# One tile of a depthwise convolution's 31 taps moved from VectorE to GpSimd

## The chip, the cores and the metric

The kernel runs on one core of one Trainium2 chip. The metric is the device time of one execution in microseconds; several executions are made and the median is quoted. The profiled execution is one more of them, with its own time. In the profile PE is TensorE, DVE is VectorE, ACT is ScalarE, POOL is GpSimd and SP is SyncE, whose queue issues the weight transfers.

## The reference, cut to what matters

The program computes two transformer-like blocks on 256 tokens of width 1024. The first block has two layers (DEPTH = 2), each a mixer and a feed-forward part. The mixer joins an mLSTM branch (four heads) with a convolution branch; the convolution branch is what the change touches:

```python
a = glu_a * jax.nn.sigmoid(glu_b)
a = causal_depthwise_conv(a, w_dw, b_dw)            # 31 taps, each channel by itself
a = jax.nn.silu(group_layer_norm(a, N_CONV_GROUPS, g_cn, b_cn))
return jnp.concatenate([h_m, a], axis=-1) @ w_out   # h_m: the mLSTM branch, gated
```

Output t of a channel is its bias plus the sum over back = 0..30 of weight(back) times input t - back. The second block (attention, a merge, and a retrieval of experts' rows by index) follows and is not touched but for the names of some semaphores.

## The kernel before, in words

Everything is float32. Activations are held with channels on the 128 partitions and the 256 tokens along a row, so 1024 channels are eight tiles of 128x256. Weights stream through a ring of four 1 MB buffers filled by the SP queue. Each engine runs a list of instructions written out by hand in the order of the source, and semaphores join them; nothing reorders them.

U is a buffer of 32 tiles. In a mixer, U[16..23] first hold glu_a and U[24..31] the sigmoid of glu_b. `long_conv(l, pair)` (line 1461) is VectorE's work on two tiles: one multiplication makes the gated input in U[24..] for both (line 1466), and then for each of the 31 taps `tap` (line 1446) issues one instruction per tile. Tap 0 is a TENSOR_SCALAR (line 1453), taps 1 to 30 are SCALAR_TENSOR_TENSOR (line 1456): shifted input times a per-channel weight plus the running sum, written back to U[16..]. Each tap waits for the tap before it on the same tile, so two tiles taken in turn keep the engine from standing still. VectorE's order in a layer is: pairs 0, 1, 2 of the long convolution, the short convolution of the mLSTM branch (4 taps, 8 tiles, `short_conv`), pair 3, the gate logarithms (lines 1532 to 1537), then for each of four heads the decay weights, the scores, and a quotient written to tmp[2h, 2h+1] (line 1556), and then the norms. tmp has eight tiles; early in the layer it holds the weights wvT that TensorE reads at line 573.

TensorE meanwhile does the input projection (lines 540 and 553), the value, query and key products (594, 584), the gates (610), more projection (540), the four heads (632 to 649), the mLSTM norm (659 to 668), the first half of the output projection (678), and only then waits for the convolution (`conv_ready`) and sums its tiles for the group norm (688). ScalarE moves results out of the accumulators (1051), applies silu to the short convolution (1096), and prepares the gates (1105 to 1116).

GpSimd issues DMAs. In the second layer its list reads: the load of mem_2; a wait for the last of the heads (`head_done`); two small loads; a wait for the mixer; wgn and wcmp; and so on.

Of the kernel before, what the change touches and what calls it, by code (L numbers as in the profile page):

```python
# [12 lines left out]
P = 128  # L13
# [160 lines left out]
def build_program(nc, a, out):  # L174
    ctx = ExitStack()
    with ctx:
# [220 lines left out]
        def _(pool):  # L397
# [36 lines left out]
            pool.wait_ge(sem("mod_kept"), 5)  # L434
            pool.dma_start(memtok, a["mem_2"][0].rearrange("(s p) d -> p s d", p=P)).then_inc(sem("mem_in"), 16)
            pool.wait_ge(sem("head_done"), H * DEPTH)
            pool.dma_start(onehot[0:N_BUCKETS, :], a["onehot"]).then_inc(sem("bias_in"), 16)
# [4 lines left out]

            pool.wait_ge(sem("bias_masked"), 1)
            pool.wait_ge(sem("bias_copied"), 1)
            pool.dma_start(bias_dram.rearrange("p h u -> h p u"), bias_w[0:NH, :].unsqueeze(1).broadcast_to([NH, P, 512])).then_inc(sem("bias_out"), 16)
# [6 lines left out]
            pool.wait_ge(sem("memT_ready"), 1)  # L452
            pool.dma_start(rc, a["rcount"].partition_broadcast(P)).then_inc(sem("rcount_in"), 16)
            pool.wait_ge(sem("x_ready"), 2 * DEPTH * CT)
            pool.dma_start(wcmp[1], a["wcmp"][1]).then_inc(sem("wcmp_in"), 16)
            pool.dma_start(wpg[:, :, :], a["wpg"]).then_inc(sem("wpg_in"), 16)
            pool.wait_ge(sem("pooled"), 1)
# [22 lines left out]
        def _(pe):  # L480
# [81 lines left out]
            for l in range(DEPTH):  # L562
# [122 lines left out]

                pe.wait_ge(sem("conv_ready"), 4 * (l + 1))
                for c in range(CT):
                    i = nc.tensor.matmul(st[:, c, :], ones[:, :], U[:, 16 + c, :], start=True, stop=True)
                    if c % 2:
                        i.then_inc(sem("gn_summed"), 1)  # L690
# [24 lines left out]
                for j in range(16):  # L715
                    w = ring_slot(("w_ff2", l, j)).rearrange("p (k n) -> p k n", n=P)
                    if l == DEPTH - 1 and j == 4:
                        pe.wait_ge(sem("mem_scaled"), 1)
                        for c in range(CT):
                            for s in range(2):  # L720
                                i = nc.tensor.transpose(st[:, c, P * s:P * s + P], memtok[:, s, P * c:P * c + P], ident[:, :])
                        i.then_inc(sem("mem_turned"), 1)
                        pe.wait_ge(sem("bias_in"), 32)
                        nc.tensor.matmul(ms[1][0:NH, :, :].rearrange("p a t -> p (a t)"), rel[0:N_BUCKETS, :], onehot[0:N_BUCKETS, :],
                                         start=True, stop=True).then_inc(sem("bias_made"), 1)
                    if j % 2 == 0:
                        b = take_bank()
                    for k in range(16):
                        kk = 16 * (j % 2) + k
                        i = nc.tensor.matmul(b[:, 0, :], w[:, k, :], U[:, kk, :], start=(kk == 0), stop=(kk == 31))  # L730
                    i.then_inc(sem("slot_used"), 1)
# [140 lines left out]
            for u in range(len(UNITS)):  # L872
                if u + 1 < len(UNITS):
                    scores(u + 1)
                for name in FILL[u]:
                    if name == "mix":
                        pe.wait_ge(sem("wpg_in"), 16)
# [124 lines left out]
        def _(act):  # L1002
# [81 lines left out]
            for l in range(DEPTH):  # L1084
# [83 lines left out]
                for c in range(CT):  # L1168
                    drain_y(l, 3, c, ("w_ff2", l, 2 * c + 1))
                    if l == DEPTH - 1 and c == 1:  # L1170
# [3 lines left out]
                        i.then_inc(sem("memT_ready"), 1)  # L1174
                        act.wait_ge(sem("bias_made"), 1)
                        nc.scalar.copy(bias_w[0:NH, 0:T], ms[1][0:NH, 0, :]).then_inc(sem("bias_copied"), 1)
                norm_pair(2 * l + 1)
# [128 lines left out]
            for s in range(2):  # L1306
                act.wait_ge(sem("acc_made"), s + 1)
                link(nc.scalar.activation(h_tok[:, s, :], acc[:, s, :], ACT.Square, accum_out=mstat[:, 0, s:s + 1]))
                nc.scalar.activation(mstat[:, 1, s:s + 1], mstat[:, 0, s:s + 1], ACT.Sqrt, bias=eps_col[:, 0:1], scale=1.0 / D).then_inc(sem("tok_std"), 1)
                for hf in range(2):  # L1310
# [36 lines left out]
            for s in range(2):  # L1347
                act.wait_ge(sem("v_used"), (2 * PH - 1 + s) * TOPK)
                link(nc.scalar.activation(h_tok[:, s, :], acc[:, s, :], ACT.Square, accum_out=mstat[:, 0, s:s + 1]))
                nc.scalar.activation(mstat[:, 1, s:s + 1], mstat[:, 0, s:s + 1], ACT.Sqrt, bias=eps_col[:, 0:1], scale=1.0 / D).then_inc(sem("last_std"), 1)  # L1350

        @block.vector
        def _(dve):
# [108 lines left out]
            def long_conv(l, pair):  # L1462

                a, b = U[:, 16 + 2 * pair:18 + 2 * pair, :], U[:, 24 + 2 * pair:26 + 2 * pair, :]
                dve.wait_ge(sem("proj_drained"), 60 * l + (2 * pair + 2 if pair < 3 else 16))
                link(nc.vector.tensor_tensor(b, a, b, ALU.mult))
                for back in range(KC):
                    tap(l, U[:, 16:24], U[:, 24:32], KC, W_DW, B_DW, back, (2 * pair, 2 * pair + 1), "conv_ready" if back == KC - 1 else None)

# [47 lines left out]
            for l in range(DEPTH):  # L1517
# [22 lines left out]
                for h in range(H):  # L1540
# [13 lines left out]
                    link(nc.vector.tensor_tensor(den[:, :], den[:, :], en_b[:, :], ALU.max))  # L1554
                    link(nc.vector.reciprocal(den[:, :], den[:, :]))
                    nc.vector.tensor_tensor(tmp[:, 2 * h:2 * h + 2, :], st[:, 6:8, :], den[:, :].unsqueeze(1).broadcast_to([P, 2, T]), ALU.mult).then_inc(sem("head_done"), 1)

# [43 lines left out]
                if l == DEPTH - 1:  # L1601
# [7 lines left out]

                    nc.vector.memset(bias_w[0:NH, T:512], NEG).then_inc(sem("bias_masked"), 1)  # L1610
                sum_pair(2 * l + 1)
# [29 lines left out]
            for u, (g, s) in enumerate(UNITS):  # L1641
# [24 lines left out]
                if u == 1:  # L1666

                    dve.wait_ge(sem("pool_kept"), 1)
                    dve.wait_ge(sem("cmp_made"), 1)
                    dve.wait_ge(sem("rcount_in"), 16)  # L1670
                    src = poolT
# [41 lines left out]
            def norm_tokens(s):  # L1713

                dve.wait_ge(sem("tok_std"), s + 1)
                link(nc.vector.reciprocal(mstat[:, 1, s:s + 1], mstat[:, 1, s:s + 1]))
# [72 lines left out]
            for s in range(2):  # L1789
                dve.wait_ge(sem("last_std"), s + 1)  # L1790
                link(nc.vector.reciprocal(mstat[:, 1, s:s + 1], mstat[:, 1, s:s + 1]))
# [27 lines left out]
```

## Time and profile before

| what | value |
|---|---|
| median of three runs | 2181.64 us (2178.7 to 4809.78) |
| profiled execution, its own time | 2180.84 us |
| its span, first to last instruction | 2179.1 us |
| PE busy | 1952.1 us (90% of the span) |
| DVE busy | 1050.0 us (48%) |
| ACT busy | 491.5 us (23%) |
| POOL busy | 314.1 us (14%) |
| mean granted TensorE clock | 0.966 of full speed |

Between the span and the execution's own time lie 1.7 us. A share of busy time is an average over very different stages: in the first half of the program TensorE works nearly without a gap, in the last third the row transfers of the retrieval set the pace. What an edit in one stage is worth is read from that stage.

### The profile page before, as it was taken

Reading aid. Unit: us, or ns where it says so; the run is one execution under the profiler, and the core shown is the slowest. Engines: PE = TensorE matmul, PEld = TensorE weight load, DVE = VectorE, ACT = ScalarE, POOL = GpSimd, SP = SyncE. Lnnn points to the kernel's source line nnn. Section 1 sums busy time; section 2 is a strip of 40 time slices with the busy share of each in tenths; the row PEclk is TensorE's granted clock in tenths of the full one; section 3 lists DMA queues with packets and bytes.
Section 4 is the critical chain, followed back from the end, with each engine's and each line's share of the span. In section 5 each row is a group of like instructions: output and inputs, shape, how many; then the busy total and the mean of one; then the engine's idle time right before and its main releaser. Section 6 shows DMA issues by size and latency. Waiting matters only on the chain.

```text
span 2179.1 us, 20885 instructions
## 1 busy us (share of the span) xinstructions
PE 1952.1 (90%) x7920; PEld 1433.0 (66%) x7920; DVE 1050.0 (48%) x2553; ACT 491.5 (23%) x1198; POOL 314.1 (14%) x328
## 2 busy tenths in 40 slices
PE   4998899999999899999999999998887888888776
PEld 4877688888786687888888777787443433433332
DVE  6993566500796422001200322223777767677754
ACT  2023221100113222120010344312213213222222
POOL 1000001000000000000000000001444344344441
PEclk9999899999999999999999999999999999999999
DMA  9712169944341143449542222245999999999996
GB/s 401 277 57 78 42 267 414 377 151 148 134 188 39 40 177 117 155 140 248 206 155 97 107 78 77 78 155 225 392 423 421 421 421 413 414 422 421 421 421 283
DMA packets 71715, 517.38 MB, mean 237 GB/s; under 512 B 8128, under 2 KB 8384, under 8 KB 11456
## 3 DMA queue, kind: packets, MB, share of 16 engines
q0 software_dynamic: 45808, 326.65, 37.6%
q1 hardware_dynamic: 25808, 189.40, 23.1%
q8 instruction: 63, 1.03, 0.2%
q14 instruction: 36, 0.29, 0.0%
HBM read 510.78 MB, written 5.24 MB: 237 GB/s over the span
## 4 chain that ended last, share of the span: by engine, by line
PE 71%; DMA 13%; DVE 10%; ACT 4%; issue 1%; SPq 0%; POOL 0%; DVEq 0%; ACTq 0%; POOLq 0%
PE pj L540 17%; DMA region<-in_peer_uv,small 10%; PE pj L730 9%; PE pj L745 9%; PE st L997 8%; PE pj L678 5%; DVE region L1778 3%; PE pj L553 3%; PE pj L965 2%; PE pj L584 1%; PE pj L757 1%; PE pj L774 1%; PE pj L864 1%; DMA pe_T<-in_pe_cols 1%; DMA ring<-in_ring_w 1%
## 5 line engine op out<-in xcount | busy, mean ns | idle before, releaser
L997 PE MATMUL st<-region 128*128 128x512 f32 x940 | 447.4, 625 | 118.3 <-ACT region L1340 118.2
L997 PEld LDWEIGHTS st<-region 128*128 128x128 f32 x940 | 179.9, 198 | 375.2 <-issue 196.2
L540 PE MATMUL pj<-hT,ring 128*128 128x256 f32 x1792 | 392.9, 381 | 1.0 <-ACT region L1159 1.0
L540 PEld LDWEIGHTS pj<-hT,ring 128*128 128x128 f32 x1792 | 340.9, 191 | 49.1 <-ACT region L1159 1.8
L1778 DVE CUSTOM_DVE_ANT_0 region<-region 128x1024 f32<-128x1024 f32 x235 | 285.6, 1224 | 107.1 <-DMA region<-in_peer_uv,small 104.0
L475 POOL DMA_INDIRECT region<-in_peer_uv,small x235 | 254.8, 1084 | 394.7 <-PE st L997 328.7
L730 PE MATMUL pj<-region,ring 128*128 128x256 f32 x1024 | 222.1, 379 | 3.6 <-ACT region L1159 2.7
L730 PEld LDWEIGHTS pj<-region,ring 128*128 128x128 f32 x1024 | 194.2, 190 | 31.9 <-ACT region L1159 3.5
L1456 DVE SCALAR_TENSOR_TENSOR region<-region,pc 128x255 f32<-128x255 f32 (+19 forms) x528 | 202.8, 473 | 0.0
L1340 ACT ACTIVATE region<-ident,small 128x128 f32<-128x128 f32 x256 | 88.8, 394 | 381.6 <-DVE small L1786 381.6
L1408 DVE TENSOR_TENSOR tmp<-xT,hT 128x256 f32<-128x256 f32 x32 | 13.6, 425 | 260.0 <-ACT hT L1072 260.0
L1482 DVE CUSTOM_DVE_ANT_0 region<-region 128x1024 f32<-128x1024 f32 x96 | 113.0, 1222 | 53.4 <-DMA region<-in_ada_rest 40.2
L745 PE MATMUL pj<-hT,ring 128*128 128x256 f32 x576 | 128.8, 384 | 0.6 <-ACT region L1249 0.6
L745 PEld LDWEIGHTS pj<-hT,ring 128*128 128x128 f32 x576 | 109.9, 192 | 16.3 <-issue 1.2
L678 PE MATMUL pj<-region,ring 128*128 128x256 f32 x448 | 106.5, 402 | 4.9 <-DVE region L1568 4.9
L678 PEld LDWEIGHTS pj<-region,ring 128*128 128x128 f32 x448 | 90.8, 204 | 21.1 <-issue 7.2
L1051 ACT ACTIVATE region<-pj 128x512 f32<-128x512 f32 x56 | 33.5, 597 | 225.1 <-PE pj L540 173.4
L553 PE MATMUL pj<-hT,ring 128*128 128x256 f32 x256 | 64.3, 418 | 18.2 <-ACT hT L1064 18.2
L432 POOL DMA_DIRECT2D region<-in_ada_rest x40 | 21.4, 535 | 384.2 <-DVE mod_sum L1482 362.2
L1072 ACT ACTIVATE hT<-pj,mod_scale 128x256 f32<-128x256 f32 x30 | 14.2, 474 | 275.1 <-PE pj L730 204.6
L553 PEld LDWEIGHTS pj<-hT,ring 128*128 128x128 f32 x256 | 54.1, 213 | 29.7 <-issue 21.0
L745 PE MATMUL pj<-region,ring 128*128 128x256 f32 x320 | 70.2, 380 | 2.6 <-DVE region L1636 1.9
(321 smaller groups left out, 1958.6 us busy)
## 6 DMA issues: line engine op xcount, KB each, us to landing
ring<-in_ring_w SPq DMA_DIRECT2D x161, 1024.0 KB, 4.8
region<-in_ada_rest POOLq DMA_DIRECT2D x40, 1024.0 KB, 12.3
region<-in_ada_first SPq DMA_DIRECT2D x4, 2048.0 KB, 17.6
region<-in_wqkv SPq DMA_DIRECT2D x2, 3072.0 KB, 12.2
region<-in_wcmp POOLq DMA_DIRECT2D x2, 2048.0 KB, 8.6
bias_dram<-region POOLq DMA_DIRECT2D x1, 4096.0 KB, 46.5
region<-in_peer_uv,small POOLq DMA_INDIRECT x235, 16.5
tmp<-in_wvT SPq DMA_DIRECT2D x2, 1024.0 KB
```

What stands on the lines that cost most here:

```text
L475: nc.gpsimd.indirect_dma_start(out=uv[n % NBUF], out_offset=None, in_=a["peer_uv"], in_offset=bass.IndirectOffsetOnAxis(ap=ids[:, n:n + 1] ...
L540: i = nc.tensor.matmul(b[:, m, :], w[:, k, P * m:P * m + P], hT[:, k, :], start=(k == 0), stop=(k == CT - 1))
L553: i = nc.tensor.matmul(b[:, m, :], w[:, k, P * m:P * m + P], hT[:, k, :], start=(k == 0 and m == 0), stop=(k == CT - 1 and m == 1))
L678: i = nc.tensor.matmul(b[:, 0, :], w[:, k, :], U[:, 8 + k, :], start=(k == 0), stop=(k == 15))
L730: i = nc.tensor.matmul(b[:, 0, :], w[:, k, :], U[:, kk, :], start=(kk == 0), stop=(kk == 31))
L745: i = nc.tensor.matmul(b[:, n, :], w[:, k, P * m:P * m + P], src[:, k, :], start=(k == 0), stop=(k == k_tiles - 1))
L965: i = nc.tensor.matmul(b[:, m, :], w[:, k, P * m:P * m + P], hT[:, k, :], start=(k == 0), stop=(k == CT - 1))
L997: i = nc.tensor.matmul(acc[:, u % 2, 512 * hf:512 * hf + 512], diag[:, m % NDIAG, :], uv[m % NBUF][:, D + 512 * hf:D + 512 * hf + 512], st ...
L1340: nc.scalar.activation(diag[:, m % NDIAG, :], ident[:, :], ACT.Copy, scale=wgt[:, u, k:k + 1]).then_inc(sem("diag_ready"), 1)
L1456: i = nc.vector.scalar_tensor_tensor(dst[:, c, back:T], src[:, c, 0:T - back], wc, dst[:, c, back:T], ALU.mult, ALU.add)
L1482: nc.vector.tensor_tensor_reduce(w, w, c_act, 1.0, 0.0, ALU.mult, ALU.add, mod_sum[:, ada_at:ada_at + 1]).then_inc(sem("ada_used"), 1)
L1778: nc.vector.tensor_tensor_reduce(row, row, h_tok[:, u % 2, :], 1.0, 0.0, ALU.mult, ALU.add, dots[:, u, k:k + 1]).then_inc(sem("u_used"), 1)
```

## The change: what it does

In the second layer (l = 1) the long convolution of tile 5 is taken out of VectorE's pair 2 and done on GpSimd. VectorE still multiplies the gated input for both tiles of the pair and then signals `glu_ready`; its taps of that pair are those of tile 4 alone. GpSimd has no fused form here: tap 0 is one TENSOR_SCALAR, and each of taps 1 to 30 is a product into tmp[7] (TENSOR_SCALAR) and an addition to U[21] (TENSOR_TENSOR), with a wait on GpSimd's own semaphore between each instruction and the next. GpSimd starts when `glu_ready` has come and TensorE has finished with wvT in tmp (`wvg_made`). Two waits on the end of this work are new: VectorE's last head quotient, which overwrites tmp[7], and TensorE's group sums. The other edits join pairs of semaphores into one; in one of them VectorE, in the second block, now waits for the load of wpg as well as for that of rcount (`pool_in` at 32).

```diff
@@ gpsimd, after the load of mem_2
+            pool.wait_ge(sem("glu_ready"), 1)
+            pool.wait_ge(sem("wvg_made"), DEPTH)
+            l, c = DEPTH - 1, 5
+            for back in range(KC):
+                wc = pc[:, l, W_DW + (KC - 1 - back) * CT + c:W_DW + (KC - 1 - back) * CT + c + 1]
+                if back == 0:
+                    nc.gpsimd.tensor_scalar(U[:, 16 + c, :], U[:, 24 + c, :], wc, pc[:, l, B_DW + c:B_DW + c + 1], ALU.mult, ALU.add).then_inc(sem("pool_tap"), 1)
+                    continue
+                pool.wait_ge(sem("pool_tap"), back)
+                nc.gpsimd.tensor_scalar(tmp[:, 7, back:T], U[:, 24 + c, 0:T - back], wc, None, ALU.mult).then_inc(sem("pool_product"), 1)
+                pool.wait_ge(sem("pool_product"), back)
+                nc.gpsimd.tensor_tensor(U[:, 16 + c, back:T], U[:, 16 + c, back:T], tmp[:, 7, back:T], ALU.add).then_inc(sem("pool_conv_ready" if back == KC - 1 else "pool_tap"), 1)
             pool.wait_ge(sem("head_done"), H * DEPTH)
@@ tensor, before the group sums
                 pe.wait_ge(sem("conv_ready"), 4 * (l + 1))
+                if l == DEPTH - 1:
+                    pe.wait_ge(sem("pool_conv_ready"), 1)
@@ vector, long_conv
-                link(nc.vector.tensor_tensor(b, a, b, ALU.mult))
+                i = nc.vector.tensor_tensor(b, a, b, ALU.mult)
+                tiles = (2 * pair, 2 * pair + 1)
+                if l == DEPTH - 1 and pair == 2:
+                    link_to(i, "glu_ready", 1)
+                    tiles = tiles[:1]
+                else:
+                    link(i)
                 for back in range(KC):
-                    tap(l, U[:, 16:24], U[:, 24:32], KC, W_DW, B_DW, back, (2 * pair, 2 * pair + 1), "conv_ready" if back == KC - 1 else None)
+                    tap(l, U[:, 16:24], U[:, 24:32], KC, W_DW, B_DW, back, tiles, "conv_ready" if back == KC - 1 else None)
@@ vector, the heads' quotient
+                    if l == DEPTH - 1 and h == H - 1:
+                        dve.wait_ge(sem("pool_conv_ready"), 1)
                     nc.vector.tensor_tensor(tmp[:, 2 * h:2 * h + 2, :], st[:, 6:8, :], den[:, :].unsqueeze(1).broadcast_to([P, 2, T]), ALU.mult).then_inc(sem("head_done"), 1)
@@ vector, the second block
-                    dve.wait_ge(sem("rcount_in"), 16)
+                    dve.wait_ge(sem("pool_in"), 32)
```

On GpSimd the work comes between the load of mem_2 and the load of onehot. In a row stand the line, the operation, what it writes and reads (tmp, and region, of which U is a part) and what it waits for. Before:

```order
24 L435 DMA region<-in_mem 128x2x1024 [waits mod_kept]
25 L437 DMA region<-in_onehot 32x512 [waits head_done]
26 L438 DMA region<-in_rel_bias 32x16
27 L440 DMA small<-in_wgn 128x384 [waits mix_ready]
28 L441 DMA region<-in_wcmp 128x4096
```

After, its beginning and its end (rows 30 to 82 repeat the pair of product and addition, one element shorter each time):

```order
24 L435 DMA region<-in_mem 128x2x1024 [waits mod_kept]
25 L442 TENSOR_SCALAR region<-region,pc 128x256 [waits wvg_made,glu_ready]
26 L445 TENSOR_SCALAR tmp<-region,pc 128x255 [waits pool_tap]
27 L447 TENSOR_TENSOR region<-region,tmp 128x255 [waits pool_product]
28 L445 TENSOR_SCALAR tmp<-region,pc 128x254 [waits pool_tap]
29 L447 TENSOR_TENSOR region<-region,tmp 128x254 [waits pool_product]
...
84 L445 TENSOR_SCALAR tmp<-region,pc 128x226 [waits pool_tap]
85 L447 TENSOR_TENSOR region<-region,tmp 128x226 [waits pool_product]
86 L449 DMA region<-in_onehot 32x512 [waits head_done]
87 L450 DMA region<-in_rel_bias 32x16
88 L452 DMA small<-in_wgn 128x384 [waits mix_ready]
```

So 61 instructions stand in a chain of waits ahead of the load of onehot. On VectorE pair 2 of the second layer read before:

```order
609 L1466 TENSOR_TENSOR region<-region 128x512 [waits proj_drained]
610 L1453 TENSOR_SCALAR region<-region,pc 128x256 [waits dve_step]
611 L1453 TENSOR_SCALAR region<-region,pc 128x256
612 L1456 SCALAR_TENSOR_TENSOR region<-region,pc 128x255 [waits dve_step] x2
613 L1456 SCALAR_TENSOR_TENSOR region<-region,pc 128x254 [waits dve_step] x2
```

and now, with the last head's quotient that waits for GpSimd:

```order
609 L1479 TENSOR_TENSOR region<-region 128x512 [waits proj_drained]
610 L1466 TENSOR_SCALAR region<-region,pc 128x256 [waits glu_ready]
611 L1469 SCALAR_TENSOR_TENSOR region<-region,pc 128x255 [waits dve_step]
612 L1469 SCALAR_TENSOR_TENSOR region<-region,pc 128x254 [waits dve_step]
...
732 L1577 TENSOR_TENSOR tmp<-st,small 128x512 [waits pool_conv_ready,dve_step]
```

Each tap is now one instruction that waits for the one just ahead of it, where there were two in turn.

## Rows read from the trace of the kernel before

**Rows 1.** The page: span, and shares of the chain that ended last, by engine.

```profile
span 2179.1 us, 20885 instructions
PE 71%; DMA 13%; DVE 10%; ACT 4%; issue 1%; SPq 0%; POOL 0%; DVEq 0%; ACTq 0%; POOLq 0%
```

**Rows 2.** The chain that ended last, second mixer: start us, us, what ran.

```profile
566.94 55.34 PE pj L540 x256
...
635.42 13.83 PE pj L540 x64
...
651.86 14.10 PE pj L584 x64
...
666.63 10.54 PE ms L610 x48
...
686.06 1.28 ACT L1114
...
735.45 1.76 DVE small L1555
737.23 0.69 DVE tmp L1556
```

**Rows 3.** Timeline of DVE: start, us, line, operation, [idle before <-releaser].

```profile
593.55 0.73 DVE L1453 TENSOR_SCALAR region<-region,pc 128x256 f32<-128x256 f32 x2
...
618.36 22.87 DVE L1456 SCALAR_TENSOR_TENSOR region<-region,pc 128x255 f32<-128x255 f32 x60
641.14 0.74 DVE L1453 TENSOR_SCALAR region<-region,pc 128x256 f32<-128x256 f32 x2
...
653.18 0.70 DVE L1466 TENSOR_TENSOR region<-region 128x512 f32<-128x512 f32 x1
...
654.56 22.89 DVE L1456 SCALAR_TENSOR_TENSOR region<-region,pc 128x255 f32<-128x255 f32 x60
682.80 0.41 DVE L1532 SCALAR_TENSOR_TENSOR region<-region 4x256 f32<-4x256 f32 x1 [5.35 <-ACT region L1111]
...
685.33 0.40 DVE L1537 TENSOR_TENSOR region<-region 4x256 f32<-4x256 f32 x1
...
700.22 0.42 DVE L1553 TENSOR_TENSOR small<-small,st 128x256 f32<-128x256 f32 x1
700.67 0.42 DVE L1554 TENSOR_TENSOR small<-small 128x256 f32<-128x256 f32 x1
```

**Rows 4.** Timeline of ACT, same columns.

```profile
649.27 0.60 ACT L1051 ACTIVATE region<-pj 128x512 f32<-128x512 f32 x1 [6.31 <-PE pj L540]
649.89 1.28 ACT L1096 ACT_TABLE_LOAD   x1
...
656.12 0.62 ACT L1096 ACTIVATE region<-region 128x512 f32<-128x512 f32 x1
```

**Rows 5.** Timeline of POOL, same columns.

```profile
3.11 0.29 POOL L407 TENSOR_SCALAR_AFFINE_SELECT ident<-ident 128x128 f32<-128x128 f32 x1 [0.24 <-POOL small L405]
3.36 0.61 POOL L410 TENSOR_SCALAR_AFFINE_SELECT causal<-causal 128x512 f32<-128x512 f32 x1
3.93 0.28 POOL L413 TENSOR_SCALAR_AFFINE_SELECT to_row<-to_row 128x64 f32<-128x64 f32 x1
```

**Rows 6.** Timeline of POOL, the retrieval stage: two issues of row transfers.

```profile
1590.03 0.94 POOL L475 DMA_INDIRECT region<-in_peer_uv,small  x1 [0.54 <-PE st L997]
1591.74 1.81 POOL L475 DMA_INDIRECT region<-in_peer_uv,small  x1 [0.78 <-PE st L997]
```

**Rows 7.** Timeline of DVE, the same moment.

```profile
1591.53 1.22 DVE L1778 CUSTOM_DVE_ANT_0 region<-region 128x1024 f32<-128x1024 f32 x1
```

**Rows 8.** Start of line 573 in PE's timeline; after it wvT is free.

```profile
623.02 3.71 PE L573 MATMUL ms<-wg,tmp 128*128 128x8 f32 x32 [0.73 <-issue]
```

**Rows 9.** POOL's load of wpg, DVE's first use of rcount, and time to landing.

```profile
1073.02 0.54 POOL L456 DMA_DIRECT2D small<-in_wpg  x1
...
1229.04 1.43 DVE L1682 TENSOR_TENSOR tmp<-tmp,region 128x256 f32<-128x256 f32 x4
...
small<-in_wpg POOLq DMA_DIRECT2D x1, 256.0 KB, 8.9
```

More of the change, by code:

```diff
@@ L441, in _ @@
             pool.dma_start(wcmp[0], a["wcmp"][0]).then_inc(sem("wcmp_in"), 16)
-            pool.wait_ge(sem("bias_masked"), 1)
-            pool.wait_ge(sem("bias_copied"), 1)
+            pool.wait_ge(sem("bias_rows"), 2)
             pool.dma_start(bias_dram.rearrange("p h u -> h p u"), bias_w[0:NH, :].unsqueeze(1).broadcast_to([NH, P, 512])).then_inc(sem("bias_out"), 16)
@@ L452, in _ @@
             pool.wait_ge(sem("memT_ready"), 1)
-            pool.dma_start(rc, a["rcount"].partition_broadcast(P)).then_inc(sem("rcount_in"), 16)
+            pool.dma_start(rc, a["rcount"].partition_broadcast(P)).then_inc(sem("pool_in"), 16)
             pool.wait_ge(sem("x_ready"), 2 * DEPTH * CT)
             pool.dma_start(wcmp[1], a["wcmp"][1]).then_inc(sem("wcmp_in"), 16)
-            pool.dma_start(wpg[:, :, :], a["wpg"]).then_inc(sem("wpg_in"), 16)
+            pool.dma_start(wpg[:, :, :], a["wpg"]).then_inc(sem("pool_in"), 16)
             pool.wait_ge(sem("pooled"), 1)
@@ L724, in _ @@
                         nc.tensor.matmul(ms[1][0:NH, :, :].rearrange("p a t -> p (a t)"), rel[0:N_BUCKETS, :], onehot[0:N_BUCKETS, :],
-                                         start=True, stop=True).then_inc(sem("bias_made"), 1)
+                                         start=True, stop=True).then_inc(sem("mem_turned"), 1)
                     if j % 2 == 0:
@@ L876, in _ @@
                     if name == "mix":
-                        pe.wait_ge(sem("wpg_in"), 16)
+                        pe.wait_ge(sem("pool_in"), 32)
                         pe.wait_ge(sem("pooled"), 1)
@@ L1174, in _ @@
                         i.then_inc(sem("memT_ready"), 1)
-                        act.wait_ge(sem("bias_made"), 1)
-                        nc.scalar.copy(bias_w[0:NH, 0:T], ms[1][0:NH, 0, :]).then_inc(sem("bias_copied"), 1)
+                        act.wait_ge(sem("mem_turned"), 2)
+                        nc.scalar.copy(bias_w[0:NH, 0:T], ms[1][0:NH, 0, :]).then_inc(sem("bias_rows"), 1)
                 norm_pair(2 * l + 1)
@@ L1308, in _ @@
                 link(nc.scalar.activation(h_tok[:, s, :], acc[:, s, :], ACT.Square, accum_out=mstat[:, 0, s:s + 1]))
-                nc.scalar.activation(mstat[:, 1, s:s + 1], mstat[:, 0, s:s + 1], ACT.Sqrt, bias=eps_col[:, 0:1], scale=1.0 / D).then_inc(sem("tok_std"), 1)
+                nc.scalar.activation(mstat[:, 1, s:s + 1], mstat[:, 0, s:s + 1], ACT.Sqrt, bias=eps_col[:, 0:1], scale=1.0 / D).then_inc(sem("row_std"), 1)
                 for hf in range(2):
@@ L1349, in _ @@
                 link(nc.scalar.activation(h_tok[:, s, :], acc[:, s, :], ACT.Square, accum_out=mstat[:, 0, s:s + 1]))
-                nc.scalar.activation(mstat[:, 1, s:s + 1], mstat[:, 0, s:s + 1], ACT.Sqrt, bias=eps_col[:, 0:1], scale=1.0 / D).then_inc(sem("last_std"), 1)
+                nc.scalar.activation(mstat[:, 1, s:s + 1], mstat[:, 0, s:s + 1], ACT.Sqrt, bias=eps_col[:, 0:1], scale=1.0 / D).then_inc(sem("row_std"), 1)
         @block.vector
@@ L1608, in _ @@
                     dve.wait_ge(sem("bias_in"), 32)
-                    nc.vector.memset(bias_w[0:NH, T:512], NEG).then_inc(sem("bias_masked"), 1)
+                    nc.vector.memset(bias_w[0:NH, T:512], NEG).then_inc(sem("bias_rows"), 1)
                 sum_pair(2 * l + 1)
@@ L1713, in norm_tokens @@
             def norm_tokens(s):
-                dve.wait_ge(sem("tok_std"), s + 1)
+                dve.wait_ge(sem("row_std"), s + 1)
                 link(nc.vector.reciprocal(mstat[:, 1, s:s + 1], mstat[:, 1, s:s + 1]))
@@ L1789, in _ @@
             for s in range(2):
-                dve.wait_ge(sem("last_std"), s + 1)
+                dve.wait_ge(sem("row_std"), s + 3)
                 link(nc.vector.reciprocal(mstat[:, 1, s:s + 1], mstat[:, 1, s:s + 1]))
```

## The prediction, blind

> **What bounds the kernel now.** I read the page first, then the chain of waits through the second mixer, then the timelines of VectorE, ScalarE and GpSimd there. The page gives the span, 2179.1 us, and the chain that ended last: 71% of it TensorE, 10% VectorE [rows 1]. An average says nothing of one convolution, so the chain through the second mixer is what counts. The reader is to see which VectorE work is in it. From 635.42 the chain runs over TensorE's projection (13.83 us), the query and key products from 651.86 (14.10 us), the gate products from 666.63 (10.54 us), ScalarE's exponential at 686.06 and then the four heads, which end with VectorE's quotient at 737.23 [rows 2]. No tap of the long convolution stands in it. VectorE is nonetheless busy without a pause from 618 to 677: pair 2's 60 later taps from 618.36, the short convolution from 641.14, pair 3's product at 653.18 and its taps from 654.56, which take 22.89 us and end at 677.45. Then it idles 5.35 us until ScalarE releases it at 682.80 [rows 3]. That idle time is the cover under which all of this convolution lies.
>
> **What is removed, and what it is worth.** Pair 2's later taps are 60 instructions in 22.87 us, 0.38 us each from start to start, although one lasts 473 ns [rows 1, 3]: two tiles in turn overlap. A single tile can't, since each tap waits for the one before. Two chained instructions of this size start 700.67 - 700.22 = 0.45 us apart at a duration of 0.42, so the hop costs 0.03 [rows 3]; a tap of 0.47 then takes about 0.50 to 0.51. The thirty taps take 15.3 us in place of 22.9, tap 0 is about 0.3 shorter: VectorE saves **7.9 us**, not half of the pair's work. Pair 2 ends near 633.3 in place of 641.1.
>
> Where do these 7.9 us go? The short convolution starts earlier, but its reader is ScalarE's silu, which has to drain the projection first: that drain starts at 649.27, released by TensorE [rows 4]. TensorE's products at 651.86 wait for that and not for VectorE. Nothing is gained there. Pair 3 could start at 653.2 - 7.9 = 645.3, but its product waits for the same drain (end 649.87), so 3.3 us of the saving go here: it would end at 649.9 + 24.3 = 674.2. Then VectorE waits for 682.80 as before, 8.6 us in place of 5.35. The gain on the path is **0**; the cover is TensorE's and ScalarE's gate chain. Were that cover gone, the gain could be 3.3 us at most.
>
> **What is added on GpSimd.** The chain of 61 instructions starts when TensorE is done with wvT, 623.02 + 3.71 = 626.73 [rows 8]; `glu_ready`, at pair 2's product before 618.36, is earlier. It has to end before VectorE's last quotient at 737.23 [rows 2]: 110.5 us, or **1.81 us an instruction**. The trace has no TENSOR_SCALAR or TENSOR_TENSOR on GpSimd. The nearest rows are its selects, which read one tensor and write one: 128 elements a row take 0.25 us from start to start (3.11 to 3.36), 512 take 0.57 (3.36 to 3.93) [rows 5], so 0.83 ns an element and 0.14 us fixed. A product of 256 elements is then 0.36 us. For the addition, with its second input, I add another 256 x 0.83 ns: 0.57 us. The hop through GpSimd's own semaphore is bounded above by 0.24 us, the idle time before the first select [rows 5], and below by 0. The sum is 31 x 0.36 + 30 x 0.57 + 60 x 0 to 0.24 = 28.3 to 42.7 us, an end between **655 and 669**. From above: the dearest GpSimd instruction in the trace is the issue of row transfers, 0.94 us, at times 1.81 [rows 6]. 61 at 0.94 + 0.24 end at 699, 61 at 1.81 + 0.24 at 752. I take the selects, which are elementwise work of the same kind; the far end stays for the range. With it the new waits on `pool_conv_ready`, at VectorE's quotient and at TensorE's group sums some 20 us later, find the work done 68 us earlier and cost nothing. What is queued behind it on GpSimd (the onehot load and all after) waited for the heads anyway, so it moves only if the quotient does.
>
> **The rest.** `pool_in` adds a wait for wpg: issued at 1073.02 and landed 8.9 us later, near 1082, where VectorE's first instruction behind that wait starts at 1223.87 [rows 9]. 142 us of cover, cost nothing. The other joined semaphores count the same events.
>
> **The sum** against the profiled execution (2180.84 us) is 0; that execution stands 0.8 below the median of the three runs, so I forecast that median and a few tenths for collisions: **2182 us**.
>
> **Rival 1: GpSimd holds VectorE up** (slower). VectorE's taps have two tensor inputs in SBUF, and so has GpSimd's addition. If the two engines take turns at reading, every GpSimd instruction may stop VectorE for its whole duration: 31 x 0.36 + 30 x 0.57 = 28.3 us. Without that, VectorE's work to the end of pair 3 is continuous to 677.45 - 7.9 = 669.6; the gate chain can take it as late as 683.1 (682.80, and 0.3 more since line 1537 ends at 685.73 and ScalarE begins its exponential only at 686.06 [rows 2, 3]). So 13.5 us are free, 0.22 us for each of 61 instructions; above that, the heads start late and everything behind them too. Full blocking gives 669.6 + 28.3 - 683.1 = 14.8 us, a median of **2196**; a TensorE that stands idle longer may add 1 to 3. Against it: in the retrieval GpSimd writes transfer descriptors while VectorE reads two inputs, and VectorE's 1224 ns there equal the 1222 of line 1482, where GpSimd does little [rows 1]. There it was GpSimd that stretched, from 0.94 to 1.81 us, at 1591.74 when VectorE had started at 1591.53 [rows 6, 7]. If that is what happens here, each of 61 is stretched by 0.87: 42.7 + 53.1 = 95.8 us, an end at 722.5, still ahead of 737.23. But descriptors are written and not read, so the row is not the same case.
>
> The Trainium skill (SBUF — State Buffer, "Who interferes with whom") states that a VectorE instruction with two SBUF inputs contends with a GpSimd instruction that reads SBUF, and that the one that starts second is blocked for the whole of the other. By that rule the sum would be this rival's 2196 if VectorE is mostly second, and 2182 if GpSimd is. No row of the trace shows the case: the stretched issue at 1591.74 agrees on who loses there, and not on what is shared.
>
> **Rival 2: GpSimd comes late** (slower). Above 1.81 us an instruction all told, the last quotient waits, and TensorE, ScalarE and the onehot load behind it. At 2.0 us the chain ends at 748.7 and the loss is 11.5 us, **2193**; at the far end above (752) 15 us, 2197. For it: two instructions, two hops and a possible stretch in each tap; against it: the selects say 0.7.
>
> **Rival 3: a gain.** The change doesn't do what it is worth on paper if the freed 7.9 us shorten nothing, which is my forecast; the opposite is that something there hung on VectorE after all. Its bound is the idle time that TensorE has at 651.86 behind ScalarE, 651.86 - (635.42 + 13.83) = 2.6 us [rows 2]: **2179**. The timeline names another cause for it.
>
> **How the numbers follow.** Hidden entirely, or with up to 3 us of collisions in the heads: 0.58. Rival 1: 0.25, spread from 2184 to 2200. Rival 2: 0.12, most of it between 2184 and 2200, with a tail that goes far. Rival 3: 0.05. The likeliest case's own range is 2179 to 2185. For 8 in 10 the range takes in the rivals' bulk: **2178 to 2198**; outside lie half of rival 3, rival 2's tail and the edge of rival 1. A measurement of this kernel can tell about 2%, 44 us, from no change. Faster by that: 0.01. Slower by that needs GpSimd at (737.23 + 44 - 626.73) / 61 = 2.5 us an instruction: 0.04. Within 2%: 0.95.
>
> **What would show it.** GpSimd's chain should start near 627 and its product and addition start 0.4 to 0.8 us apart, ending before 700. VectorE's pair 2 should be 15 to 16 us long and its taps in pair 3 still 0.38 us apart; wider taps than that are rival 1, and then line 1532 (now 1553) no longer waits for ScalarE. A wait of the last quotient for GpSimd is rival 2. The chain that ended last should hold no GpSimd work. I would be wrong if a GpSimd product costs several times a select, or if taps in pair 3 stretch beyond 0.6 us.

## The result, and the profile after

The changed kernel takes 2185.94 us (median of 8, 2182.77 to 2187.87) against 2181.2 for the kernel before (median of 8; one of its executions took 4809.78 and bears on nothing). The ratio is 1.0022, 95% interval 1.0012 to 1.0032: slower by some 5 us (2.6 to 7.0 by the interval), and far less than the 2% that counts as a difference here. Each profiled execution drifts by a few microseconds against another long before the changed place, so stages are compared from a common event: the start of VectorE's first product of the long convolution in the second layer (568.65 before, 565.36 after).

The page of the changed kernel: the chain that ended last, by engine and by line, and the group of taps (busy, mean ns | idle before).

```profile
PE 66%; DVE 15%; DMA 14%; ACT 4%; issue 1%; SPq 0%; POOL 0%; DVEq 0%; ACTq 0%; POOLq 0%
PE pj L551 13%; DMA region<-in_peer_uv,small 11%; PE pj L743 9%; PE pj L758 9%; PE st L1010 8%; DVE region L1469 5%; PE pj L689 5%; DVE region L1799 3%; PE pj L564 3%; PE pj L978 2%; PE pj L770 1%; PE pj L787 1%; PE pj L877 1%; DMA pe_T<-in_pe_cols 1%; DMA ring<-in_ring_w 1%
...
L1469 DVE SCALAR_TENSOR_TENSOR region<-region,pc 128x255 f32<-128x255 f32 (+22 forms) x498 | 210.6, 496 | 1.1
```

VectorE's share of the chain rose from 10% to 15% [rows 1], and the taps (line 1469, which was 1456) now stand in it with 5%. There are 30 taps fewer, and they are busy for longer. The timeline of VectorE in the changed kernel shows where (start, us, line, operation, [idle before <-releaser]):

```profile
565.36 0.69 DVE L1479 TENSOR_TENSOR region<-region 128x512 f32<-128x512 f32 x1 [11.84 <-ACT region L1064]
...
614.85 16.68 DVE L1469 SCALAR_TENSOR_TENSOR region<-region,pc 128x255 f32<-128x255 f32 x30
631.46 1.13 DVE L1466 TENSOR_SCALAR region<-region,pc 128x256 f32<-128x256 f32 x2
632.51 3.72 DVE L1469 SCALAR_TENSOR_TENSOR region<-region,pc 128x255 f32<-128x255 f32 x6
...
652.18 32.79 DVE L1469 SCALAR_TENSOR_TENSOR region<-region,pc 128x255 f32<-128x255 f32 x60
684.89 0.41 DVE L1551 SCALAR_TENSOR_TENSOR region<-region 4x256 f32<-4x256 f32 x1
...
687.41 0.41 DVE L1556 TENSOR_TENSOR region<-region 4x256 f32<-4x256 f32 x1
...
737.72 0.69 DVE L1577 TENSOR_TENSOR tmp<-st,small 128x512 f32<-128x512 f32 x1
```

Pair 3's 60 taps take 32.79 us in place of 22.89, and line 1551 no longer waits for ScalarE, where it waited 5.35 us [rows 3]. That is the sign the prediction named for its first rival (it calls the line 1553; in the changed kernel the line of 1532 is 1551). GpSimd in the changed kernel, the first instructions and the last:

```profile
623.65 0.80 POOL L442 TENSOR_SCALAR region<-region,pc 128x256 f32<-128x256 f32 x1 [197.79 <-PE ms L584]
624.54 0.97 POOL L445 TENSOR_SCALAR tmp<-region,pc 128x255 f32<-128x255 f32 x1
625.59 0.77 POOL L447 TENSOR_TENSOR region<-region,tmp 128x255 f32<-128x255 f32 x1
626.46 0.96 POOL L445 TENSOR_SCALAR tmp<-region,pc 128x254 f32<-128x254 f32 x1
...
678.89 0.66 POOL L447 TENSOR_TENSOR region<-region,tmp 128x226 f32<-128x226 f32 x1
738.70 0.59 POOL L449 DMA_DIRECT2D region<-in_onehot  x1 [59.14 <-DVE tmp L1577]
```

A product and an addition take 1.92 us together at first, hops included (624.54 to 626.46), and the chain ends at 679.55, 58 us ahead of the quotient at 737.72. GpSimd is not late; nobody waits for it. No run here tries an instruction on GpSimd that would do both for two tensors.

ScalarE, which takes up the gate logarithms, before and (second block) after:

```profile
685.44 0.60 ACT L1051 ACTIVATE region<-pj 128x512 f32<-128x512 f32 x1 [1.38 <-PE pj L540]
686.06 1.28 ACT L1114 ACT_TABLE_LOAD   x1
687.35 0.41 ACT L1114 ACTIVATE small<-region 4x256 f32<-4x256 f32 x1
```

```profile
682.77 1.28 ACT L1127 ACT_TABLE_LOAD   x1
687.85 0.42 ACT L1127 ACTIVATE small<-region 4x256 f32<-4x256 f32 x1 [3.80 <-DVE region L1556]
```

The row at 686.06 [rows 2], which the prediction takes for the exponential, is a table load. It follows ScalarE's own drain of an accumulator and does not wait for VectorE: before, line 1537 had ended at 685.73, and the exponential began at 687.35, 1.62 us later. Now the load is long done when VectorE delivers at 687.82; ScalarE stands idle 3.80 us and begins 0.03 us after it.

**The account.** From the common event VectorE's pair 3 ends at 684.97 - 565.36 = 119.6 us. Undisturbed it would end at 100.8: the 108.8 of before (677.45 - 568.65), less 8.0 that the single tile saves (24.2 us from pair 2's product to the short convolution before, 16.2 in the second experiment below). So VectorE was stretched by **18.8 us** while 61 GpSimd instructions ran, 0.31 each. Its last gate instruction starts 122.05 us after the event in place of 116.68, +5.4; the 1.6 us of slack at ScalarE give 1.6 back, and the last quotient starts at 172.36 in place of 168.58, **+3.8 us**, which lies inside the 2.6 to 7.0 of the runs.

The two profiled executions differ by more than that behind the quotient. From the event to the last instruction they take 1617.8 us after and 1610.5 before, +7.4, so 3.6 us are lost behind it. They go with TensorE's clock: from 750 to 775 the granted clock is 0.84 after and 0.91 before, from 775 to 800 it is 0.88 and 0.95, that is, TensorE spends more of these stretches at its lower level of 1.2 GHz in place of 2.4. Just before, from 738 to 750, TensorE waited for the norm and was busy for only 7.5 of 12 us after and 7.1 before. Whether the change makes such stretches longer or these two executions merely differ is open; the third experiment below comes back to it.

The prediction reads four more rows of the kernel before. It cites the first three under [rows 1], and the last, the first instruction behind the wait for rcount, under [rows 9]:

```profile
L1778 DVE CUSTOM_DVE_ANT_0 region<-region 128x1024 f32<-128x1024 f32 x235 | 285.6, 1224 | 107.1 <-DMA region<-in_peer_uv,small 104.0
...
L1456 DVE SCALAR_TENSOR_TENSOR region<-region,pc 128x255 f32<-128x255 f32 (+19 forms) x528 | 202.8, 473 | 0.0
...
L1482 DVE CUSTOM_DVE_ANT_0 region<-region 128x1024 f32<-128x1024 f32 x96 | 113.0, 1222 | 53.4 <-DMA region<-in_ada_rest 40.2
```

```profile
1223.87 0.17 DVE L1674 COPY tmp<-region 128x4 f32<-128x4 f32 x1 [9.78 <-ACTq L1263]
```

### The profile page after: what moved, and what is told of

Same layout as the page of the kernel before. It is cut to its first block, busy times and chain, and to the rows that moved or that the text cites. A ratio compares the mean times of both kernels' runs of the same rounds, so it can differ in the third digit from the quotient of the medians.

```text
span 2183.2 us, 20917 instructions
## 1 busy us (share of the span) xinstructions
PE 1952.9 (89%) x7920; PEld 1433.3 (66%) x7920; DVE 1058.4 (48%) x2522; ACT 491.3 (23%) x1198; POOL 366.8 (17%) x389
## 4 chain that ended last, share of the span: by engine, by line
PE 66%; DVE 15%; DMA 14%; ACT 4%; issue 1%; SPq 0%; POOL 0%; DVEq 0%; ACTq 0%; POOLq 0%
PE pj L551 13%; DMA region<-in_peer_uv,small 11%; PE pj L743 9%; PE pj L758 9%; PE st L1010 8%; DVE region L1469 5%; PE pj L689 5%; DVE region L1799 3%; PE pj L564 3%; PE pj L978 2%; PE pj L770 1%; PE pj L787 1%; PE pj L877 1%; DMA pe_T<-in_pe_cols 1%; DMA ring<-in_ring_w 1%
## 5 line engine op out<-in xcount | busy, mean ns | idle before, releaser
L1469 DVE SCALAR_TENSOR_TENSOR region<-region,pc 128x255 f32<-128x255 f32 (+22 forms) x498 | 210.6, 496 | 1.1
L758 PEld LDWEIGHTS pj<-hT,ring 128*128 128x128 f32 x576 | 109.9, 192 | 16.2 <-issue 1.2
L432 POOL DMA_DIRECT2D region<-in_ada_rest x40 | 21.3, 534 | 382.1 <-DVE mod_sum L1501 360.2
```

The source lines that it names most:

```text
L758: i = nc.tensor.matmul(b[:, n, :], w[:, k, P * m:P * m + P], src[:, k, :], start=(k == 0), stop=(k == k_tiles - 1))
L1469: i = nc.vector.scalar_tensor_tensor(dst[:, c, back:T], src[:, c, 0:T - back], wc, dst[:, c, back:T], ALU.mult, ALU.add)
```

## The experiments

The theory: GpSimd's and VectorE's instructions stop each other; VectorE loses more than the 14.8 us that are free, and the gate chain starts late. The rivals: the single tile's chained taps, the new waits or joined semaphores, or a mere difference between builds.

### Everything back but the semaphores

```diff
-            (GpSimd's loop over the taps of tile 5)
+            pool.sem_inc(sem("pool_conv_ready"), 1)
@@ long_conv
-                    tiles = tiles[:1]
```

> The changed kernel with tile 5's taps back on VectorE and no work on GpSimd; the joined semaphores and the two new waits stay (they find their semaphore already counted). Theory (the two engines stop each other): pair 3's 60 later taps take 22.9 us again, VectorE waits some 5 us for ScalarE at the gate logarithms, and the time is that of the kernel before within 1.5 us. Rival (the joined semaphores or a different build cost the 4.7 us): the time stays 4 to 5 us above before.

Measured: 2180.14 us, ratio 0.9999 (0.9990 to 1.0008). Pair 3's taps take 22.87 us, VectorE waits 5.37 us, the quotient starts 168.58 us after the event, as before. Semaphores, waits and build cost nothing that can be measured; that rival falls, and with it a cost of `pool_in`.

### The saving alone

GpSimd only signals, and tile 5's convolution is left out altogether.

```diff
-            (GpSimd's loop over the taps of tile 5)
+            pool.sem_inc(sem("pool_conv_ready"), 1)
```

> Leaves out the long convolution of tile 5 in the second layer, on both engines; VectorE does tile 4 alone as in the changed kernel. Theory: the saving alone is worth nothing on the path. Pair 2's 30 chained taps take 15.3 us, pair 3 ends about 3 us earlier in its stage, VectorE's wait at the gate logarithms grows from 5.35 to about 8.6 us, and the time is that of before within 1.5 us. Rival (VectorE's convolution was on the path after all): 2 to 3 us below before. Rival (the chained taps of a single tile are what costs): above before.

Measured: 2179.1 us, ratio 0.9997 (0.9988 to 1.0006). VectorE's timeline:

```profile
618.32 15.09 DVE L1460 SCALAR_TENSOR_TENSOR region<-region,pc 128x255 f32<-128x255 f32 x30
...
650.04 0.69 DVE L1470 TENSOR_TENSOR region<-region 128x512 f32<-128x512 f32 x1 [4.59 <-ACT region L1055]
...
682.94 0.41 DVE L1542 SCALAR_TENSOR_TENSOR region<-region 4x256 f32<-4x256 f32 x1 [8.65 <-ACT region L1115]
```

The chained taps take 15.09 us, pair 3's product then waits 4.59 us for ScalarE's drain, and the wait at the gate chain is 8.65. The quotient starts 168.59 us after the event, as before. The saving is all idle time: worth nothing even if tile 5 cost nothing anywhere.

### GpSimd after VectorE's convolution

```diff
             pool.wait_ge(sem("wvg_made"), DEPTH)
+            pool.wait_ge(sem("conv_ready"), 4 * DEPTH)
```

> The changed kernel, but GpSimd starts tile 5 only when VectorE has ended pair 3 (it also waits for conv_ready at 8). Theory: pair 3's 60 taps take 22.9 us, VectorE waits again for ScalarE, and since the 61 instructions at 0.9 us or less end some 55 us later, just ahead of the last head's quotient, the time is that of before, +0 to +3 us for collisions in the heads. If the instructions are faster with VectorE mostly idle, 0.5 to 0.7 us each, they end 15 to 25 us ahead of the quotient. Rival (it is the new waits or the chain, not the overlap): +4 to +5 us as in the changed kernel; or the quotient waits for GpSimd.

Measured: 2181.3 us, ratio 1.0012 (1.0001 to 1.0023). Pair 3's taps take 22.87 us again and line 1552 waits 8.65 us for ScalarE. GpSimd's timeline, the start of its chain and its end:

```profile
671.69 0.55 POOL L443 TENSOR_SCALAR region<-region,pc 128x256 f32<-128x256 f32 x1 [246.22 <-DVE region L1470]
672.34 0.95 POOL L446 TENSOR_SCALAR tmp<-region,pc 128x255 f32<-128x255 f32 x1
673.37 0.72 POOL L448 TENSOR_TENSOR region<-region,tmp 128x255 f32<-128x255 f32 x1
...
725.51 0.66 POOL L448 TENSOR_TENSOR region<-region,tmp 128x226 f32<-128x226 f32 x1
736.13 0.59 POOL L450 DMA_DIRECT2D region<-in_onehot  x1 [9.96 <-DVE tmp L1578]
```

With the same work out of the convolution's way the quotient starts 169.19 us after the event: +0.6 where it was +3.8. What stays there is collisions in the gate chain and the heads. VectorE in them:

```profile
681.26 0.76 DVE L1554 TENSOR_TENSOR region<-small,region 4x256 f32<-4x256 f32 x1
...
710.05 0.80 DVE L1574 TENSOR_TENSOR small<-small 128x256 f32<-128x256 f32 x1
```

Undisturbed these take 0.41 and 0.42. The chain ends at 726.17, 9.0 us ahead of the quotient at 735.14. The hope that the instructions would take 0.5 to 0.7 us with VectorE mostly idle was wrong for the product, which still takes 0.93.

The whole execution shows less of this than the quotient does. By the ratio some 2.6 us are lost (0.2 to 5.0), against 4.8 in the changed kernel, and the two intervals overlap. The eleven executions fall into groups: five from 2179.2 to 2180.6, two near 2181.6, four from 2184.6 to 2185.3, and the profiled one is the slowest. It loses its time behind the quotient: from the event to its last instruction it takes 1617.7 us, 7.2 more than before, of which 6.6 come after the quotient, and the granted clock from 738 to 750 is 0.75 (0.86 before) and from 750 to 775 0.84 (0.91). GpSimd does nothing there that it didn't do before. So the delay at the quotient is shown to be the overlap with the convolution; how much of the 5 us of the whole belongs to it, and how much to stretches at the lower clock behind it, is not settled.

### Half a dose

```diff
-            for back in range(KC):
+            for back in range(16):
@@ the addition's signal
-... "pool_conv_ready" if back == KC - 1 ...
+... "pool_conv_ready" if back == 15 ...
```

Taps 16 to 30 of tile 5 are left out.

> The changed kernel with GpSimd's chain cut after tap 15 (31 instructions in place of 61; taps 16 to 30 of tile 5 are left out). In the changed kernel VectorE's stretch from pair 2's taps to pair 3's end is 70.6 us where its parts undisturbed sum to 52.1: 18.5 us for 61 instructions, 0.30 each. Theory: 31 of them cost 9.4 us, less than the 13.5 us that are free, so VectorE waits again for ScalarE by 3 to 5 us and the time is that of before within 1.5 us. Rival (any overlap costs on the path, in proportion): +2.4 us.

Measured: 2180.26 us, ratio 0.9999 (0.9990 to 1.0008). Pair 3 ends 109.8 us after the event, 9.0 more than undisturbed, 0.29 for each of 31 instructions (9.4 was expected). VectorE waits 7.62 us for ScalarE; TensorE had a lower granted clock in this profiled execution (0.91 from 625 to 685, 0.97 before), so ScalarE was about 3.3 us later than usual, and without that the wait would be 4.3. The quotient of this execution starts 171.57 us after the event, +3.0, all of it within that delay. The loss is not in proportion: below the free time the eleven executions lose nothing (-2.2 to +1.7 us), where proportion wanted 2.4.

### The contention without the saving

```diff
-                    tiles = tiles[:1]
@@ gpsimd: all three U[:, 16 + c, ...] become
+                tmp[:, 6, ...]
```

> VectorE does all taps as in the kernel before; GpSimd does the 61 instructions of tile 5 as well, with its sum in tmp[6] where nothing reads it. So the contention is there and the saving is not. Theory: VectorE is stretched by 61 x 0.30 = 18.5 us between pair 2 and the end of pair 3, of which 5.65 are free: 12.9 us on the path, a time of 2194. Rival (VectorE was stretched in the changed kernel because a single tile's taps are chained): less than 5 us.

Measured: 2192.17 us, ratio 1.0060 (1.0044 to 1.0077). Pair 3 ends 126.8 us after the event, 18.0 more than the 108.8 of before; the quotient starts 181.86 after it, +13.3 for the 12.9 that were expected. That agreement is partly luck: the 1.6 us of slack at ScalarE were not counted, and GpSimd's last instructions, which ran into the gate chain, cost about as much there (its six instructions start over 4.20 us, 691.90 to 696.10, in place of 2.53). The rival of the chained single tile falls: here every pair has two tiles. GpSimd's timeline holds a surprise:

```profile
623.50 17.60 POOL L442 TENSOR_SCALAR tmp<-region,pc 128x256 f32<-128x256 f32 x1 [197.01 <-PE ms L584]
641.19 1.10 POOL L445 TENSOR_SCALAR tmp<-region,pc 128x255 f32<-128x255 f32 x1
642.37 0.73 POOL L447 TENSOR_TENSOR tmp<-tmp 128x255 f32<-128x255 f32 x1
```

and VectorE's beside it:

```profile
614.93 22.88 DVE L1469 SCALAR_TENSOR_TENSOR region<-region,pc 128x255 f32<-128x255 f32 x60
637.73 0.73 DVE L1466 TENSOR_SCALAR region<-region,pc 128x256 f32<-128x256 f32 x2
638.38 2.45 DVE L1469 SCALAR_TENSOR_TENSOR region<-region,pc 128x255 f32<-128x255 f32 x6
640.75 0.81 DVE L1466 TENSOR_SCALAR region<-region,pc 128x256 f32<-128x256 f32 x2
641.48 3.77 DVE L1469 SCALAR_TENSOR_TENSOR region<-region,pc 128x255 f32<-128x255 f32 x6
...
656.04 35.94 DVE L1469 SCALAR_TENSOR_TENSOR region<-region,pc 128x255 f32<-128x255 f32 x60
```

Against two tiles in turn, whose taps follow without a gap, GpSimd's first instruction is held for 17.60 us, until VectorE comes to its second pair of TENSOR_SCALARs in the short convolution; the taps of that time are not stretched at all (22.88 us). Once GpSimd is in, it keeps its turns, and pair 3's 60 taps take 35.94 us. In the changed kernel the first instruction took 0.80 us (623.65): there pair 2 had one tile, with a hop between its taps. So the single tile does not only save less than half of the pair, it also lets GpSimd in sooner: its first instruction ends 59.1 us after the event, and 75.9 us after it here.

### Products, additions, memsets

Each replaces the loop on GpSimd by a chain of one kind of instruction into tmp[7], which nothing reads; VectorE does all taps.

```diff
+            for n in range(60):          # memsets: 120
+                ... wait for the instruction before, wc as for tap 30 ...
+                nc.gpsimd.tensor_scalar(tmp[:, 7, 1:T], U[:, 24 + c, 0:T - 1], wc, None, ALU.mult)          # products
+                nc.gpsimd.tensor_tensor(tmp[:, 7, 1:T], U[:, 24 + c, 1:T], U[:, 24 + c, 0:T - 1], ALU.add)  # additions
+                nc.gpsimd.memset(tmp[:, 7, 1:T], 0.0)                                                        # memsets
```

> VectorE does all taps; GpSimd runs 60 chained products (TENSOR_SCALAR with a per-partition weight, 255 elements, one tensor in) into tmp[7], which nothing reads. In the changed kernel the pattern of VectorE's single-tile taps (0.48, 0.57, 0.81 us in each 1.9 us) puts the longest pause beside the addition. Theory with two inputs as the cause: a product, with one tensor read, stretches VectorE by 0.1 to 0.2 us each. Theory of a lock for the whole instruction: by its 0.9 us or nearly, 30 us and more in all until VectorE is late.

> As the products, with 60 chained additions (TENSOR_TENSOR, 255 elements, two tensors in). Theory with two inputs as the cause: each stretches VectorE by 0.3 to 0.5 us, more than a product does. Theory of a lock for the whole instruction: by its 0.7 us.

> As the products, with 120 chained memsets of 255 elements a row, which read nothing. If what is shared is reading, VectorE is not stretched at all: pair 3's 60 taps in 22.9 us, and 5 us of waiting for ScalarE. If it is the writing or the engine's issue, it is stretched.

Measured, one execution each: 2177.71, 2197.09 and 2177.68 us, beside 2180.45 of before (median of 7, 2176.93 to 2182.18). Of these times only the second stands clear of that spread; the rest is read from the traces. Pair 3's taps with products, additions and memsets, with some rows around them, from VectorE's timeline in each kernel:

```profile
656.92 25.65 DVE L1465 SCALAR_TENSOR_TENSOR region<-region,pc 128x255 f32<-128x255 f32 x60
```

```profile
638.21 1.39 DVE L1462 TENSOR_SCALAR region<-region,pc 128x256 f32<-128x256 f32 x2
639.52 4.64 DVE L1465 SCALAR_TENSOR_TENSOR region<-region,pc 128x255 f32<-128x255 f32 x6
...
664.02 31.81 DVE L1465 SCALAR_TENSOR_TENSOR region<-region,pc 128x255 f32<-128x255 f32 x60
695.75 0.41 DVE L1546 SCALAR_TENSOR_TENSOR region<-region 4x256 f32<-4x256 f32 x1
```

```profile
639.91 0.96 DVE L1462 TENSOR_SCALAR region<-region,pc 128x256 f32<-128x256 f32 x2
...
643.15 0.80 DVE L1462 TENSOR_SCALAR region<-region,pc 128x256 f32<-128x256 f32 x2
...
653.82 22.86 DVE L1465 SCALAR_TENSOR_TENSOR region<-region,pc 128x255 f32<-128x255 f32 x60
681.56 0.41 DVE L1546 SCALAR_TENSOR_TENSOR region<-region 4x256 f32<-4x256 f32 x1 [4.88 <-ACT region L1120]
```

Counted from the event to the end of pair 3, the additions cost VectorE 130.1 - 108.8 = 21.3 us, 0.36 each. The products cost 4.8 us; 32 of them ended in that time, so 0.15 each, and that fits the free time: the quotient starts at 168.61, as before. The 120 memsets cost 0.5 us in all, the taps nothing. So it is instructions that read a tensor which cost the taps time, and the addition, with two tensors to read, costs more than the product, though it is the shorter of the two. That the second read is the reason is the likeliest account; these chains differ in their operation as well. With the additions six taps take 4.64 us, 0.76 each, and the 59 additions behind the first take 0.74 each from start to start (from 638.8, when the first ended, to 682.5): one tap for one addition, by turns.

Two tensor inputs on VectorE are not needed for a stretch. Its TENSOR_SCALARs, which read one tensor and per-channel weights, take 0.73 us a pair before, 1.39 beside the additions, and 0.96 (the first pair) to 0.80 beside the memsets, which makes up all of the 0.5 us that the memsets cost. Why they feel even the memsets, no run here shows.

The group of the products in two stretches of GpSimd's time (busy, mean ns | idle before), first under pair 3's taps from 657 to 680, then from 683 to 725 with VectorE mostly idle:

```profile
L443 POOL TENSOR_SCALAR tmp<-region,pc 128x255 f32<-128x255 f32 x18 | 21.4, 1190 | 1.7
```

```profile
L443 POOL TENSOR_SCALAR tmp<-region,pc 128x255 f32<-128x255 f32 x28 | 26.9, 960 | 2.6
```

GpSimd pays too: 0.23 us a product.

The prices do not add up in the mixed chain: 30 additions at 0.36, 30 products at 0.15 and tap 0 come to 15.5 us, and 18.8 were measured. The other 3.3 us stay open.

### What makes a product long

The same chain of 60 with the constant 0.5 for the weight; with tap 0's form, weight and bias; and of all 256 elements without a shift.

```diff
-                nc.gpsimd.tensor_scalar(tmp[:, 7, 1:T], U[:, 24 + c, 0:T - 1], wc, None, ALU.mult)
+                nc.gpsimd.tensor_scalar(tmp[:, 7, 1:T], U[:, 24 + c, 0:T - 1], 0.5, None, ALU.mult)
+                nc.gpsimd.tensor_scalar(tmp[:, 7, 1:T], U[:, 24 + c, 0:T - 1], wc, bias, ALU.mult, ALU.add)
+                nc.gpsimd.tensor_scalar(tmp[:, 7, :], U[:, 24 + c, :], wc, None, ALU.mult)
```

> 60 chained GpSimd products as before, by the constant 0.5 in place of a per-partition weight. A product took 0.93 us with VectorE idle where tap 0 (product and sum, two weights per partition) took 0.55 and an addition 0.70. If the read of the weight is what costs, a product by a constant falls to 0.5 us or below.

> The same 60 chained instructions in tap 0's form: times a weight, plus a bias, both per partition, shifted by one element. If it is the form with one operation that is slow, 0.55 us each as tap 0; if the shift or the odd size, 0.93. VectorE is stretched by each of them as by a product, by 0.1 to 0.2 us, or less if the instruction holds what is shared for less time.

> The same 60 products with one weight, but of all 256 elements and without a shift. If shift or odd size made the product slow, 0.55 us each; if the form with one operation, 0.93.

Measured, one execution each: 2183.01, 2179.13 and 2179.74 us, beside a single 2177.51 of before, too few to tell these times apart. The shortest instruction of each kind took 0.86 us by a constant, 0.57 in tap 0's form, 0.92 without the shift. So it is the form with one operation that is slow; a product and a sum in one instruction take 0.57 us, the product alone 0.93. The longest of each was again the first, 15.1 to 17.6 us. Under pair 3 the taps took 28.33, 27.73 and 25.76 us. The product by a constant is the shorter one and costs VectorE more: 8.9 us for 48 that ended by the end of pair 3, 0.19 each; the reason is open. That tap 0's form, being shorter, might hold VectorE up less did not come true: 44 ended beside the taps and cost 7.2 us in all, 0.16 each, where 32 of the unshifted products cost 4.9, 0.15 each.

## Why the prediction was right and where it was wrong

The time lies in the range of 2178 to 2198, and the change is within 2% as forecast. The likeliest case did not happen, though: neither the 2182 us nor its own range to 2185 nor its mechanism, work hidden entirely. Its first rival did happen, which had a chance of 0.25. That the forecast holds is owed to a range that took the rivals in, and to VectorE's 14.8 free us, which swallowed most of a stretch of 18.8.

- **The saving and its worth**: right. 7.9 us were forecast and 8.0 measured (taps 15.09 us for 15.3); a gain of 0 was shown by leaving tile 5 out. The prediction says that 3.3 us of the saving go to the wait for the drain; by its own numbers (649.87 - 645.3) it is 4.6, and 4.59 were measured. The 3.3 us are what is left, and its sum uses them so.
- **The cover**: right in kind. VectorE's free time was put at 13.5 us. The rows make it 14.8: what it took for ScalarE's exponential at 686.06 is the table load, and the exponential comes 1.3 us later. Half a dose stayed under it, the whole went over.
- **GpSimd's speed**: mis-sized. 0.36 and 0.57 us from the selects, measured 0.93 and 0.70; a chain of 28 to 43 us was 55.9. The select was a poor neighbour for the product, which costs 2.6 times its 0.36. It did not matter for the deadline, since 110 us were there. The hop is mostly 0.08 to 0.10 us. The first product and addition start 1.05 us apart (624.54, 625.59), where 0.4 to 0.8 was named as the sign.
- **The step that failed**: that collisions between GpSimd and VectorE would stay inside the cover. Pair 3's taps were to start 0.38 us apart and start 0.55 us apart (32.79 us for 60). The prediction leaned on the retrieval, where VectorE's instructions keep their 1.22 us and GpSimd's issue stretches. That row was no witness: the memsets show that one kind of GpSimd instruction leaves VectorE's two-input work alone while another stretches it, and the issue of a transfer is neither a product nor an addition. What it reads or writes no run here shows. The price of the rival was mis-sized as well, though its point of decision was right: not the whole duration (28.3 us by the selects; 49.0 by the durations measured in the third experiment) but 0.36 an addition and 0.15 a product in chains of one kind, 0.31 on average in the mixed chain, 18.8 us in all. That 28.3 is not further off is luck: the durations were put too low and the blocked share too high. 18.8 - 14.8 = 4.0, and 3.8 us were seen at the quotient.
- **What the rule said.** The Trainium skill (SBUF — State Buffer, "Who interferes with whom") states that a VectorE instruction with two SBUF inputs contends with a GpSimd instruction that reads SBUF and not with one that only writes it. The runs agree: 120 memsets left the taps at 22.86 us. The Trainium skill also calls the sharing an exclusive lock, under which the second is blocked for the whole of the first. There the measurement decides otherwise in two ways: an addition of 0.67 us costs a tap 0.36, and GpSimd can be held for 15 to 18 us, many instructions long, until a pair of TENSOR_SCALARs comes in VectorE's stream.
- **Lateness and the queues**: right. The chain ended 58 us ahead of the quotient, `pool_in` cost nothing that the first experiment could measure, and the load of onehot still waits for VectorE's quotient.

No version here beats the kernel before: the work that was moved had no worth on the path, so the best that this move can reach is a tie.

## What to carry to other kernels

Before moving work to free an engine, look at what that engine waits for next: where it idles at the end of the stretch, the freed time only makes the idle time longer. GpSimd and VectorE are not independent when both read on-chip buffers; in kernels like this one charge VectorE 0.15 to 0.36 us for every reading GpSimd instruction of 255 elements a row that runs beside taps with two tensor inputs, and compare the sum with VectorE's idle time in that stage. If work must lie on GpSimd, start it when VectorE's stream is over: that took the delay at the quotient from 3.8 to 0.6 us.

## What the runs showed of the hardware that was not expected

- GpSimd's first reading instruction was held 14.8 to 17.6 us by a gapless stream of VectorE taps in six kernels, and by chained taps hardly at all (0.80 us, where it takes 0.55 undisturbed). It got in at the first pair of TENSOR_SCALARs of the short convolution in four of them and at the second in the two whose first instruction has tap 0's form. No memset of the 120 took more than 0.74 us.
- After it is in, GpSimd gets a turn for each of its instructions, even under the same gapless stream.
- The stretch is not the duration: a product of 0.93 us costs the taps 0.15, an addition of 0.67 costs them 0.36.
- VectorE's one-tensor TENSOR_SCALARs are stretched as well, and slightly even by memsets (0.73 us a pair to 0.80).
- On GpSimd, 255 elements times a weight plus a bias take 0.57 us, times a weight alone 0.93, times a constant 0.86, the addition of two tensors 0.61 to 0.72, a memset 0.31.
